# Two fp32r activation halves in one 512-column matmul

## The chip, the cores and the metric

The kernel runs on one core of one Trainium2 chip. The metric is the time of one execution on the device in microseconds; the median of three runs of the kernel before is 2723.91 us (2716.98 to 2725.1).

## The reference

Two transformer blocks of depth 2 follow each other on 256 tokens of width 1024, in fp32. The first has a pooling and gating mixer in its layer 0 and sparse attention with retention in layer 1. The second has adaptive normalisation (nine rows of shifts, scales and gates for each layer, from a vector `c` times `ada_w`), differential attention in layer 0 and grouped attention in layer 1, and carries a second stream, the context, beside x. Every mixer stands between linear layers, and FFNs do most of the work:

```python
def swiglu_2(h, w_in, w_out):
    gate, up = jnp.split(h @ w_in, 2, axis=-1)
    return (jax.nn.silu(gate) * up) @ w_out

def half_ffn(h, m, k, g_pre, g_post, w_in, w_out):
    y = swiglu_2(modulated_norm(h, g_pre, m, k), w_in, w_out)
    return gated_residual(h, y, g_post, m, k, 0.5)
```

The hidden width is 2816. x goes through six FFNs (called gu0 to gu5 below), the context through three (gu2, gu3, gu4).

## The kernel before

**The split product.** Features lie on the 128 partitions and the 256 tokens (`T`) along the free axis. TensorE multiplies in fp32r, which keeps fewer bits than fp32, so each fp32 operand is split in a high part (rounded to fp32r) and a low part (the rest), and a product is the sum of three: high by high, high by low, low by high. `product` (L264) issues one matmul: `w` picks high or low weights (`WHI`, `WLO`), `xp` the high or low activations (`S.HN` or `S.G`, two tensors each). `three` issues the three for each of the k tiles of 128 features, one after the other into the same 256 columns of a PSUM bank. Three such matmuls are called a triple here.

**Weights.** A block is 128 x 2048: eight k tiles of two output tiles of 128 features. SyncE loads blocks into four raw slots in the order of `plan`; a load waits until the block four places ahead is done. `splits` (L223, L230, L243) lets ScalarE copy a raw block to `WHI` (three buffers) and VectorE subtract it in two halves to give `WLO`. The split of block n+2 or n+3 is issued in the middle of block n, between its two output tiles.

**Lanes.** x and the context are two lanes (`X`, `C`), generators whose steps a hand-written scheduler puts in one order: each engine runs its instructions in that order. Beside them a third generator, `modulation`, makes the shifts and gains from 72 blocks of `ada_w` (L1115, L1129). In gu5 x is alone; in the other FFNs context or modulation blocks stand between x's blocks.

**An FFN of x.** For each of 11 pairs (256 hidden features) a gate block goes to bank 0 (both output tiles side by side) and an up block to bank 1. ScalarE takes tanh of the gate bank to `TMP` (L446), VectorE forms the gate (L448), which frees the bank, then multiplies by the up bank (L461), which frees that; ScalarE writes the high part of the result to `GX_hi` (L465), VectorE the low part (L467). The first pair is made by `first_blocks`, which starts while the norm is still making the high and low parts, tile by tile: for each k the two products on the high activations, one tile later that on the low ones, and from k = 5 on the second block as well. The down projection takes, for each pair of output tiles, 22 k tiles in three blocks of 6, 8 and 8, into the first halves of two banks.

**Outputs.** `put_out` takes each of the eight output tiles of a down or output projection (`ev_out`, `od_out`, `da_out`, `ga_out`): ScalarE squares it twice and copies it to `Y`, each with the PSUM bank as its input (L352, L355, L356), and VectorE adds up the sums for the norm (L366 to L372). Then `norm` makes the inverse root with small matmuls (L538, L553) and writes `HN` (L686 to L700). Its banks are 2 and 3.

**Counts.** Input projections have 6 (ev), 14 (od, one of them with a single output tile), 12 (da) and 6 (ga) blocks for x; output projections four each; each FFN 22 gate and up blocks and 12 down blocks.

Of the kernel before, what the change touches and what calls it, by code (L numbers as in the profile page):

```python
# [9 lines left out]
P = 128  # L10
D = 1024
KD = D // P
T = 256
# [28 lines left out]
Mark = namedtuple("Mark", "sem n")  # L42

# [40 lines left out]
def build(nc, A, out):  # L84
# [4 lines left out]
    with ExitStack() as ctx:  # L89
        def sb(name, shape, dt=fp32):  # L90
            return ctx.enter_context(nc.sbuf_tensor(name, shape, dt))

        HX, HC = sb("HX", [P, KD, T]), sb("HC", [P, KD, T])
# [6 lines left out]
        with ExitStack() as g:  # L100
            HNX = [g.enter_context(nc.sbuf_tensor(f"HNX_{n}", [P, KD, T], f32r)) for n in ("hi", "lo")]
            GX = [g.enter_context(nc.sbuf_tensor(f"GX_{n}", [P, KF, T], f32r)) for n in ("hi", "lo")]
# [4 lines left out]
        HNC = [sb(f"HNC_{n}", [P, KD, T], f32r) for n in ("hi", "lo")]  # L107
        with ExitStack() as g:
            GC = [g.enter_context(nc.sbuf_tensor(f"GC_{n}", [P, 8, T], f32r)) for n in ("hi", "lo")]
# [16 lines left out]
        BANK = [ctx.enter_context(nc.psum_tensor(f"bank{n}", [P, 512], fp32)) for n in range(8)]  # L126
# [5 lines left out]
            "total", "root", "rstd", "scaled", "resid", "normed", "hn_hi", "hn_lo")]  # L132
        for n in names:
            sems[n] = ctx.enter_context(nc.semaphore(n))
# [8 lines left out]
        def carve(arena, at, end):  # L143

            def piece(n, *dims, dt=None):
# [11 lines left out]
                if len(dims) == 2:  # L157
# [5 lines left out]
                 (BANK[2], BANK[3], BANK[0], BANK[1]), (BANK[0], BANK[1]), (BANK[3], BANK[4]), BANK[2], BANK[3], False, False)  # L163
# [11 lines left out]
        def program(pe=None, act=None, dve=None, pool=None, sp=None):  # L175
# [90 lines left out]

            def three(dst, n, col, x, ks, start, stop, waits=None):
# [48 lines left out]
            def first_blocks(S, n, dst, hi, lo):  # L316


                LAG = 5
                landed(n)  # L320
                for j in range(KD + LAG):
                    for m in range(2):
                        if j < KD and on(pe, None if m else hi[j]):
                            for w in range(2):
                                product(dst[0][:, m * T:(m + 1) * T], n, m * P, j, S.HN, 0, j, w, j == 0 and m == 0 and w == 0, False, True)
                    for m in range(2):
                        if 1 <= j <= KD and on(pe, None if m else lo[j - 1]):
                            mm = product(dst[0][:, m * T:(m + 1) * T], n, m * P, j - 1, S.HN, 1, j - 1, 0, False, j == KD, True)
                            if j == KD and m == 1:
                                mm.then_inc(sems["block_done"], 1)  # L330
                    if j == LAG:
                        splits(n)
                        landed(n + 1)
                    for m in range(2):
                        for w, xp in ((0, 0), (1, 0), (0, 1)) if j >= LAG and pe else ():
                            k = j - LAG
                            mm = product(dst[1][:, m * T:(m + 1) * T], n + 1, m * P, k, S.HN, xp, k, w, k == 0 and m == 0 and (w, xp) == (0, 0),
                                         k == KD - 1 and xp == 1, True)
# [6 lines left out]
            def put_out(S, src, k, gain, *ready):  # L345

                t, first = S.tag, k == 0
                sq, gg, ev = up(f"{t}_sq"), up(f"{t}_gg"), up(f"{t}_evac")
                if on(act, *ready, *((*free.get((t, "sums"), ()), *free.get((t, "gain"), ())) if first else ())):
# [12 lines left out]
                else:  # L362
# [6 lines left out]
                    if on(dve, ev, hs0):  # L369
                        NV.tensor_tensor(part, S.H[:, k, :], S.Y[:, k, :], MUL).then_inc(hg.sem, 1)  # L370
                        dve.wait_ge(*hg)
                        NV.tensor_tensor(S.HG, S.HG, part, ADD).then_inc(hs.sem, 1)  # L372
                return ev

            def linear(S, name, blocks, dst, ready=(), first=None, gain=None):
# [3 lines left out]
                if first is not None:  # L379
# [5 lines left out]
                    first_blocks(S, n, S.pair, *first)  # L385
                for j, (b, at, *alone) in enumerate(blocks):
                    tiles = 1 if alone else 2
                    if first is None or j >= 2:
# [4 lines left out]
                        if gain is not None and not S.lag:  # L393
                            banks = S.tiles[2 * (j % 2)], S.tiles[2 * (j % 2) + 1]
                            dsts = banks[0][:, 0:T], banks[1][:, 0:T]
# [7 lines left out]
                    def job(banks=banks, at_n=at_n, at=at, tile=tile, tiles=tiles):  # L403
                        if gain is not None:
                            for m in range(2):
                                src = banks[m][:, 0:T] if not S.lag else halves(banks[m])[m]
                                free[banks[m].name] = put_out(S, src, at + m, gain, done(at_n) if m or S.lag else tile)
                            marks.append(free[banks[1].name])
# [8 lines left out]
                return marks  # L417

            def ffn(S, which, gain, first):
# [6 lines left out]
                for c, pairs in enumerate(chunks):  # L426
                    for p in pairs:
                        gate, up_ = S.pair
                        if p == 0 and not S.chunked:
                            yield ("F",)  # L430
                            n = take(t, "w_main", base)
                            take(t, "w_main", base + 1)
                            on(pe, free.get(gate.name), free.get(up_.name))
                            first_blocks(S, n, S.pair, *first)
                            ng, nu = n, n + 1
                        else:
                            yield ("D",)
                            ng = take(t, "w_main", base + 2 * p)
                            on(pe, *(first[1] if p == 0 else ()), free.get(gate.name))
                            yield from two_tiles(S, ng, halves(gate), S.HN, ALL, True, True)  # L440
                            nu = None
# [9 lines left out]
                        if nu is None:  # L451
                            yield ("D",)
                            nu = take(t, "w_main", base + 2 * p + 1)
                            on(pe, free.get(up_.name))
                            yield from two_tiles(S, nu, halves(up_), S.HN, ALL, True, True)
                        kt = 2 * p - 8 * c if S.chunked else 2 * p

                        def keep(p=p, nu=nu, kt=kt, down_done=down_done):
# [4 lines left out]
                            g = [x[:, kt:kt + 2, :].rearrange("p a b -> p (a b)") for x in S.G]  # L463
                            if on(act, ud, down_done):
                                NS.activation(g[0], S.TMP[p % 2][:, :], ACT.Copy).then_inc(hi.sem, 1)  # L465
                            if on(dve, hi):
                                NV.tensor_tensor(g[1], S.TMP[p % 2][:, :], g[0].bitcast(fp32), SUB).then_inc(lo.sem, 1)  # L467
# [7 lines left out]
                    if not S.chunked:  # L475
                        for mp in range(4):
                            banks = S.tiles[2 * (mp % 2)], S.tiles[2 * (mp % 2) + 1]
                            for cc, (k0, k1) in enumerate(SHORT_FIRST):
# [7 lines left out]
                                yield from two_tiles(S, n, [b[:, 0:T] for b in banks], S.G, ks, cc == 0, cc == 2, waits, tile, 2, mp == 3 and cc == 2)  # L486
                            for m in range(2):
                                free[banks[m].name] = put_out(S, banks[m][:, 0:T], 2 * mp + m, gain, done(n) if m else tile)
# [1597 lines left out]
```

## Time and profile before

| | |
|---|---|
| median of three runs | 2723.91 us (2716.98 to 2725.1) |
| span of the profiled execution | 2725.8 us |
| time of the profiled execution beside its span | none is given; the three runs are those above |
| instructions in it | 48854 |
| TensorE, weight loads | 93%, 88% of the span |
| VectorE, ScalarE | 63%, 46% |
| mean granted TensorE clock | 0.966 |
| read from HBM | 471.48 MB, 173 GB/s |

The span runs from the first to the last instruction. A matmul's recorded duration is longer than the distance to the next one, since matmuls are pipelined; the distance between starts is what a stream of them costs.

### The profile page before, as it was taken

The page shows a single profiled execution, that of the slowest core. Times are in us where ns is not written, and L with a number is a line of the kernel's source. Part 1 is how long each engine was busy: PE and PEld are TensorE (multiplying, and loading weights), DVE is VectorE, ACT ScalarE, POOL GpSimd, SP SyncE. Part 2 cuts the span into 40 slices and gives each one's busy share as a digit, 9 for nine tenths or more (in the row PEclk, how much of TensorE's full clock was granted, in tenths as well). Part 3 has the DMA queues.
Part 4 walks back from the last instruction along what each step waited for, and adds up shares of the span by engine and source line. Part 5 has one row for each costly group of instructions (what it writes and reads, how often), then busy time and mean ns, then how long its engine had stood idle before and what let it go on. Part 6 is the DMA issues. An engine that isn't in the chain of part 4 may idle for free.

```text
span 2725.8 us, 48854 instructions
## 1 busy us (share of the span) xinstructions
PE 2528.6 (93%) x20780; PEld 2395.9 (88%) x20780; DVE 1707.1 (63%) x2804; ACT 1248.6 (46%) x1697; POOL 1.2 (0%) x6
## 2 busy tenths in 40 slices
PE   6799997999999999999888998999999999887998
PEld 5689996888998999999887898999999999756997
DVE  6565574656766565566767576577655557646655
ACT  4443453444544444445445554455444345435443
POOL 0000000000000000000000000000000000000000
PEclk9899999999999999999898999999999999888999
DMA  6456656533555665544351344555545555363453
GB/s 218 181 200 242 241 203 229 189 109 124 186 202 216 236 226 196 211 147 154 132 174 52 120 171 154 185 175 173 179 170 179 180 177 183 114 215 137 170 178 116
DMA packets 71591, 480.14 MB, mean 176 GB/s; under 512 B 8784, under 2 KB 9296, under 8 KB 17744
## 3 DMA queue, kind: packets, MB, share of 16 engines
q1 hardware_dynamic: 66240, 468.74, 48.8%
q10 hardware_dynamic: 5136, 8.28, 1.0%
q8 instruction: 166, 2.72, 0.4%
q14 instruction: 49, 0.40, 0.0%
HBM read 471.48 MB, written 1.05 MB: 173 GB/s over the span
## 4 chain that ended last, share of the span: by engine, by line
PE 73%; DVE 13%; ACT 7%; DMA 4%; issue 3%; ACTq 0%; DVEq 0%
PE bank L264 64%; ACT whi L223 4%; DVE wlo L243 2%; DMA raw<-w_main 2%; DVE wlo L230 2%; PE bank L1115 2%; DMA raw<-w_down 1%; PE bank L997 1%; PE bank L935 1%; DVE ARX L686 1%; DVE HX L637 1%; DVE tmpx L631 1%; PE bank L985 1%; PE bank L553 0%; PE bank L1639 0%
## 5 line engine op out<-in xcount | busy, mean ns | idle before, releaser
L264 PE MATMUL bank<-HNX_hi,whi 128*128 128x256 f32 x2968 | 866.2, 293 | 64.3 <-DVE wlo L243 24.4
L223 ACT ACTIVATE whi<-raw 128x2048 fp32r<-128x2048 f32 (+1 forms) x378 | 705.5, 1868 | 334.6 <-PE bank L264 149.4
L264 PE MATMUL bank<-HNX_hi,wlo 128*128 128x256 f32 x2968 | 849.8, 287 | 0.0
L264 PE MATMUL bank<-HNX_lo,whi 128*128 128x256 f32 x2968 | 834.6, 286 | 0.0
L230 DVE TENSOR_TENSOR wlo<-raw,whi 128x1024 fp32r<-128x1024 f32 (+1 forms) x378 | 453.4, 1199 | 570.1 <-ACT whi L223 569.5
L264 PEld LDWEIGHTS bank<-HNX_hi,whi 128*128 128x128 f32 x2968 | 582.4, 196 | 91.7 <-issue 50.7
L264 PEld LDWEIGHTS bank<-HNX_hi,wlo 128*128 128x128 f32 x2968 | 583.1, 196 | 0.0
L264 PEld LDWEIGHTS bank<-HNX_lo,whi 128*128 128x128 f32 x2968 | 573.2, 196 | 1.1 <-issue 0.9
L243 DVE TENSOR_TENSOR wlo<-raw,whi 128x1024 fp32r<-128x1024 f32 (+1 forms) x378 | 450.8, 1193 | 0.0
L264 PE MATMUL bank<-HNC_hi,whi 128*128 128x256 f32 x1344 | 390.2, 290 | 11.6 <-DVE tmpc L448 4.5
L264 PE MATMUL bank<-HNC_lo,whi 128*128 128x256 f32 x1344 | 381.7, 284 | 0.0
L264 PE MATMUL bank<-HNC_hi,wlo 128*128 128x256 f32 x1344 | 381.6, 284 | 0.0
L264 PE MATMUL bank<-GX_hi,whi 128*128 128x256 f32 x1056 | 302.6, 287 | 4.0 <-DVE wlo L243 3.9
L264 PE MATMUL bank<-GX_lo,whi 128*128 128x256 f32 x1056 | 298.7, 283 | 0.0
L264 PE MATMUL bank<-GX_hi,wlo 128*128 128x256 f32 x1056 | 298.6, 283 | 0.0
L264 PEld LDWEIGHTS bank<-HNC_hi,whi 128*128 128x128 f32 x1344 | 259.2, 193 | 22.5 <-issue 7.9
L264 PEld LDWEIGHTS bank<-HNC_lo,whi 128*128 128x128 f32 x1344 | 259.4, 193 | 0.6 <-issue 0.2
L264 PEld LDWEIGHTS bank<-HNC_hi,wlo 128*128 128x128 f32 x1344 | 259.2, 193 | 0.0
L264 PEld LDWEIGHTS bank<-GX_hi,whi 128*128 128x128 f32 x1056 | 202.4, 192 | 10.4 <-DVE wlo L243 7.8
L264 PEld LDWEIGHTS bank<-GX_lo,whi 128*128 128x128 f32 x1056 | 202.5, 192 | 0.1
L264 PEld LDWEIGHTS bank<-GX_hi,wlo 128*128 128x128 f32 x1056 | 202.4, 192 | 0.0
L465 ACT ACTIVATE GX_hi<-tmpx 128x512 fp32r<-128x512 f32 x66 | 41.7, 632 | 250.0 <-DVE tmpx L461 250.0
(349 smaller groups left out, 2923.7 us busy)
## 6 DMA issues: line engine op xcount, KB each, us to landing
raw<-w_main SPq DMA_DIRECT2D x270, 1024.0 KB, 4.8
raw<-w_ada SPq DMA_DIRECT2D x72, 1024.0 KB, 4.8
raw<-w_down SPq DMA_DIRECT2D x72, 1024.0 KB, 4.9
raw<-w_down SPq DMA_DIRECT2D x36, 768.0 KB, 4.2
raw<-w_cmp SPq DMA_DIRECT2D x4, 1024.0 KB, 4.8
tmpx<-ARX ACTq DMA_DIRECT2D x18, 128.0 KB, 4.8
tmpx<-ARX ACTq DMA_DIRECT2D x32, 64.0 KB, 4.7
HX<-x_in SPq DMA_DIRECT2D x2, 512.0 KB, 6.0
```

Source lines behind the costliest of these rows:

```text
L223: NS.activation(WHI[q % HIS][:, 0:size], RAW[m % SLOTS][:, 0:size], ACT.Copy).then_inc(sems["w_hi"], 1)
L230: NV.tensor_tensor(WLO[m % SLOTS][:, 0:half], RAW[m % SLOTS][:, 0:half], WHI[q % HIS][:, 0:half].bitcast(fp32), SUB)
L243: NV.tensor_tensor(WLO[m % SLOTS][:, half:size], RAW[m % SLOTS][:, half:size], WHI[q % HIS][:, half:size].bitcast(fp32), SUB).then_inc(sem ...
L264: return NT.matmul(dst, (WHI[ordinal[n] % HIS], WLO[n % SLOTS])[w][:, k * 2 * P + col:k * 2 * P + col + P], x[xp][:, kx, :], start=start, ...
L465: NS.activation(g[0], S.TMP[p % 2][:, :], ACT.Copy).then_inc(hi.sem, 1)
L631: NV.tensor_tensor(S.TMP[k % 2][:, 0:T], S.Y[:, k, :], S.wide_y[:, 0:T], MUL).then_inc(sc.sem, 1)
L637: NV.tensor_tensor(S.H[:, k, :], S.H[:, k, :], S.TMP[k % 2][:, 0:T], ADD).then_inc(re.sem, 1)
L686: NV.scalar_tensor_tensor(S.Y[:, k, :], S.H[:, k, :], gain(k), S.wide_h[:, 0:T], MUL, MUL).then_inc(no.sem, 1)
L935: mm = NT.matmul(bank[:, c0 + c * T:c0 + (c + 1) * T], q[pr, :], k[pr, :], start=True, stop=True)
L985: mm = NT.transpose(turn_bank[:, c * P:(c + 1) * P], PB[w % 3][:, 0, c * P:(c + 1) * P], ident)
L997: mm = NT.matmul(out_bank[:, 0:P], v, PT[b][:, c * P:(c + 1) * P], start=c == 0, stop=c == len(vs) - 1)
L1115: mm = NT.matmul(bank[32 * g:32 * g + 32, 0:T], CCOL[:, k, 6 - 2 * r:38 - 2 * r], RAW[n % SLOTS][:, k * T:(k + 1) * T], start=r == 0 and k ...
```

## The change

The high and low activations become one tensor `[P, k, 2, T]`, so that for each k the two halves lie next to each other, 512 columns. For x's gate, up, down and output projections the three matmuls become two: low weights by high activations (256 columns, into a bank's first half, "main"), and high weights by both halves at once (512 columns: high by high adds to main, high by low goes to the second half, "cross"). Each output tile now has a bank of its own: gate in banks 0 and 1, up in banks 2 and 3. The norm's banks of x move to 3 and 4. Before anything else reads an output, ScalarE copies cross to SBUF and VectorE adds main to it; the instructions of old then read that sum in SBUF, and the banks are free after the add. x's input projections and everything of the context keep three matmuls. In `first_blocks` the wide matmul waits for the low half, and ahead of the second block there is a new wait, for bank 3.

```diff
+            def high_by_both(dst, n, col, k, x, kx, stop, loose=False):
+                return NT.matmul(dst, WHI[ordinal[n] % HIS][:, k * 2 * P + col:k * 2 * P + col + P], x.both[:, kx, :, :].rearrange("p a b -> p (a b)"),
+                                 start=False, stop=stop, skip_group_check=loose)
...
-                    if on(pe, *(waits or {}).get(kx, ())):
+                    if on(pe, *(waits or {}).get(kx, ())) and is_wide(dst):
+                        product(dst[:, 0:T], n, col, k, x, 0, kx, 1, start and j == 0, False, True)
+                        mm = high_by_both(dst, n, col, k, x, kx, stop and j == len(ks) - 1, True)
+                    elif pe:
                         for w, xp in ((0, 0), (0, 1), (1, 0)):
...
                     for m in range(2):
                         if j < KD and on(pe, None if m else hi[j]):
+                            if wide:
+                                product(dst[0][m][:, 0:T], n, m * P, j, S.HN, 0, j, 1, j == 0, False, True)
...
                         if 1 <= j <= KD and on(pe, None if m else lo[j - 1]):
+                            if wide:
+                                mm = high_by_both(dst[0][m], n, m * P, j - 1, S.HN, j - 1, j == KD, True)
...
                     if j == LAG:
                         splits(n)
                         landed(n + 1)
+                        on(pe, free.get(S.wide_y.name))
...
+                if not S.lag:
+                    bank, src, summed = src, S.Y[:, k, :], up("x_tile_sum")
+                    apart = up("x_cross")
+                    if on(act, *ready):
+                        NS.activation(src, bank.cross(), ACT.Copy).then_inc(apart.sem, 1)
+                    if on(dve, apart):
+                        NV.tensor_tensor(src, bank.main(), src, ADD).then_inc(summed.sem, 1)
+                    ready = (summed,)
...
+                if on(act, done(ng), held.get(p % 2)):
+                    NS.activation(made, PS[:, 0:2, T:2 * T], ACT.Copy).then_inc(gc.sem, 1)
+                if on(dve, gc):
+                    NV.tensor_tensor(gate, PS[:, 0:2, 0:T], made, ADD).then_inc(gs.sem, 1)
+                if on(act, gs):
+                    NS.activation(made, gate, ACT.Tanh, scale=0.5).then_inc(th.sem, 1)
+                if on(dve, th):
+                    NV.scalar_tensor_tensor(made, made, 1.0, gate, ADD, MUL).then_inc(act_.sem, 1)
+                free[gates[0].name] = free[gates[1].name] = gs
...
+                if on(act, done(nu)):
+                    NS.activation(up_, PS[:, 2:4, T:2 * T], ACT.Copy).then_inc(uc.sem, 1)
+                if on(dve, uc, act_):
+                    NV.tensor_tensor(up_, PS[:, 2:4, 0:T], up_, ADD).then_inc(us.sem, 1)
+                    dve.wait_ge(*us)
+                    NV.scalar_tensor_tensor(made, made, 0.5, up_, MUL, MUL).then_inc(ud.sem, 1)
+                free[ups[0].name] = free[ups[1].name] = us
```

## Rows read from the trace of the kernel before

**Rows 1.** The page: busy time by engine; the granted clock in 40 slices.

```profile
PE 2528.6 (93%) x20780; PEld 2395.9 (88%) x20780; DVE 1707.1 (63%) x2804; ACT 1248.6 (46%) x1697; POOL 1.2 (0%) x6
...
PEclk9899999999999999999898999999999999888999
```

**Rows 2.** The page's groups: count, busy us, mean ns, idle us before.

```profile
L264 PE MATMUL bank<-HNX_hi,whi 128*128 128x256 f32 x2968 | 866.2, 293 | 64.3 <-DVE wlo L243 24.4 <-ACT HNX_hi L691 16.5 <-ACT HNX_hi L689 12.8
...
L264 PE MATMUL bank<-HNC_hi,whi 128*128 128x256 f32 x1344 | 390.2, 290 | 11.6 <-DVE tmpc L448 4.5 <-DVE HNC_lo L700 4.2 <-DVE HNC_lo L842 1.4
...
L264 PE MATMUL bank<-GX_hi,whi 128*128 128x256 f32 x1056 | 302.6, 287 | 4.0 <-DVE wlo L243 3.9
```

**Rows 3.** Timeline in gu5, full clock: start us, duration us, instruction.

```profile
2590.00 0.28 PE L264 MATMUL bank<-HNX_hi,whi 128*128 128x256 f32 x1
2590.12 0.28 PE L264 MATMUL bank<-HNX_lo,whi 128*128 128x256 f32 x1
...
2590.12 0.19 PEld L264 LDWEIGHTS bank<-HNX_hi,wlo 128*128 128x128 f32 x1
```

**Rows 4.** Windows (PEclk after the engines) and timeline at the lower clock.

```profile
142.00:144.00 2.00, 2.00 (x10) 1.93 (x10) 2.00 (x7) 0.66 (x2) 0.00 (x0) 0.50 0.00 0
...
142.90 0.41 PE L264 MATMUL bank<-HNX_hi,whi 128*128 128x256 f32 x1
143.11 0.41 PE L264 MATMUL bank<-HNX_hi,wlo 128*128 128x256 f32 x1
```

**Rows 5.** Timelines of one-column matmuls and of plain fp32 matmuls, merged.

```profile
665.63 1.05 PE L793 MATMUL bank<-VEC,tmpx 128*128 128x1 f32 x8 [0.82 <-ACT tmpx L786]
666.54 0.36 PE L264 MATMUL bank<-GC_hi,whi 128*128 128x256 f32 x1
...
2412.00 0.59 PE L935 MATMUL bank<-KC,ARX 128*128 128x256 f32 x2
2412.43 0.59 PE L935 MATMUL bank<-ARX 128*128 128x256 f32 x2
```

**Rows 6.** Timeline of ScalarE and of VectorE over one pair of gu5.

```profile
2584.80 0.60 ACT L446 ACTIVATE tmpx<-bank 128x512 f32<-128x512 f32 x1 [2.60 <-PE bank L264]
2585.29 1.91 ACT L223 ACTIVATE whi<-raw 128x2048 fp32r<-128x2048 f32 x1
2591.28 0.63 ACT L465 ACTIVATE GX_hi<-tmpx 128x512 fp32r<-128x512 f32 x1 [4.08 <-DVE tmpx L461]
...
2596.32 0.60 ACT L446 ACTIVATE tmpx<-bank 128x512 f32<-128x512 f32 x1 [2.60 <-PE bank L264]
...
2585.43 0.69 DVE L448 SCALAR_TENSOR_TENSOR tmpx<-tmpx,bank 128x512 f32<-128x512 f32 x1 [0.84 <-ACT tmpx L446]
2587.23 1.23 DVE L230 TENSOR_TENSOR wlo<-raw,whi 128x1024 fp32r<-128x1024 f32 x1 [1.12 <-ACT whi L223]
2588.37 1.22 DVE L243 TENSOR_TENSOR wlo<-raw,whi 128x1024 fp32r<-128x1024 f32 x1
```

**Rows 7.** Timeline of ScalarE in gu0, with modulation blocks between.

```profile
263.48 0.60 ACT L446 ACTIVATE tmpx<-bank 128x512 f32<-128x512 f32 x1 [2.60 <-PE bank L264]
...
276.18 0.60 ACT L446 ACTIVATE tmpx<-bank 128x512 f32<-128x512 f32 x1 [2.60 <-PE bank L264]
```

**Rows 8.** Groups of 128x256 that read a bank.

```profile
L352 ACT ACTIVATE sqx<-bank 128x256 f32<-128x256 f32 x70 | 26.9, 384 | 79.1 <-PE bank L264 79.1
...
L631 DVE TENSOR_TENSOR tmpx<-ARX,bank 128x256 f32<-128x256 f32 x80 | 32.2, 413 | 2.5 <-PE bank L553 2.3
```

**Rows 9.** Timeline of TensorE after ga_out: the norm's sums.

```profile
2508.43 0.44 PE L538 MATMUL bank<-sumxy,VEC 128*32 128x64 f32 x8 [3.63 <-DVE sumxy L366]
```

**Rows 10.** Windows of gu5 and gu0 (last: DMA share, GB/s); loads, us to landing.

```profile
2520.00:2640.00 120.00, 117.98 (x975) 117.37 (x975) 73.40 (x85) 51.75 (x45) 0.00 (x0) 1.00 0.50 171
240.00:290.00 50.00, 49.68 (x440) 46.75 (x440) 26.10 (x29) 18.95 (x18) 0.00 (x0) 1.00 0.69 249
...
raw<-w_main SPq DMA_DIRECT2D x270, 1024.0 KB, 4.8
```

More of the change, by code:

```diff
@@ L42, with __getitem__, main, cross @@
 Mark = namedtuple("Mark", "sem n")
+Split = namedtuple("Split", "hi lo both")
+@dataclass
+class Bank:
+    name: str
+    ap: Any
+    def __getitem__(self, key):
+        return self.ap[key]
+    def main(self):
+        return self.ap[:, 0:T]
+    def cross(self):
+        return self.ap[:, T:2 * T]
 class Between:
@@ L125, in build @@
         ROWS = sb("rows", [P, T])
-        BANK = [ctx.enter_context(nc.psum_tensor(f"bank{n}", [P, 512], fp32)) for n in range(8)]
+        PS = ctx.enter_context(nc.psum_tensor("bank", [P, 8, 512], fp32))
+        BANK = [Bank(f"bank{n}", PS[:, n, :]) for n in range(8)]
         sems = {}
@@ L319, in first_blocks @@
                 LAG = 5
+                wide = is_wide(dst[0][0])
                 landed(n)
@@ L372, in put_out @@
                         NV.tensor_tensor(S.HG, S.HG, part, ADD).then_inc(hs.sem, 1)
+                if not S.lag:
+                    free[bank.name] = summed
                 return ev
@@ L384, in linear @@
                         on(pe, free.get(b.name))
-                    first_blocks(S, n, S.pair, *first)
+                    first_blocks(S, n, [halves(b) for b in S.pair], *first)
                 for j, (b, at, *alone) in enumerate(blocks):
@@ L428, in ffn @@
                         gate, up_ = S.pair
[L429 to L441, printed above, removed]
+                        if not S.chunked:
+                            yield from wide_pair(S, p, base, first, gain, held, lo_marks)
+                            continue
+                        yield ("D",)
+                        ng = take(t, "w_main", base + 2 * p)
+                        on(pe, *(first[1] if p == 0 else ()), free.get(gate.name))
+                        yield from two_tiles(S, ng, halves(gate), S.HN, ALL, True, True)
                         def silu(p=p, ng=ng):
@@ L450, in ffn @@
                         after(S, silu)
[L451 to L456, printed above, removed]
+                        yield ("D",)
+                        nu = take(t, "w_main", base + 2 * p + 1)
+                        on(pe, free.get(up_.name))
+                        yield from two_tiles(S, nu, halves(up_), S.HN, ALL, True, True)
+                        kt = 2 * p - 8 * c
                         def keep(p=p, nu=nu, kt=kt, down_done=down_done):
@@ L476, in ffn @@
                         for mp in range(4):
[L477 removed]
+                            banks = S.tiles[mp % 2]
                             for cc, (k0, k1) in enumerate(SHORT_FIRST):
@@ L485, in ffn @@
                                 tile = up(f"{t}_tile") if cc == 2 else None
-                                yield from two_tiles(S, n, [b[:, 0:T] for b in banks], S.G, ks, cc == 0, cc == 2, waits, tile, 2, mp == 3 and cc == 2)
+                                yield from two_tiles(S, n, [b[:, :] for b in banks], S.G, ks, cc == 0, cc == 2, waits, tile, 2, mp == 3 and cc == 2)
                             for m in range(2):
-                                free[banks[m].name] = put_out(S, banks[m][:, 0:T], 2 * mp + m, gain, done(n) if m else tile)
+                                put_out(S, banks[m], 2 * mp + m, gain, done(n) if m else tile)
                         continue
```

81 lines of the change are left out of this document (62 added, 19 removed).

## Prediction

> **What bounds the kernel now.** I read the page first: TensorE is busy 93% of the span, VectorE 63%, ScalarE 46%, and the granted clock is nine tenths or more in all but six of its 40 slices [rows 1]. The groups by line then show that one line, the split product, holds nearly all matmuls, that they come in equal thirds, and that the idle time ahead of them is small: 64.3 us ahead of the largest group, 11.6 and 4.0 ahead of two others [rows 2]. So in most stretches TensorE's own pace sets the time. What is that pace? The timeline inside a dense stretch shows a new 256-column matmul every 0.12 us, each with a weight load of its own [rows 3]. The stretch has the full clock, 2.4 GHz; 256 columns at one column per cycle are 106.7 ns, so each matmul costs 13.3 ns over its columns. What these 13.3 ns hang on decides this change.
>
> **What is removed, and what one triple gains.** A triple (three loads, three 256-column matmuls, 768 columns) becomes a pair (two loads, 256 + 512 columns, again 768 columns). No column is saved: only a load and what is paid per matmul. Triples that change: the x down projections, 1056, and of the 2968 over HNX all but those of the input projections, which keep the old form: 6+14+12+6 blocks of 16, less 8 of a half block, 600. That leaves 2368 + 1056 = 3424. At the lower clock level the pitch is 0.21 us, which is just 256 columns at 1.2 GHz, so nothing is saved there [rows 4]; I take 5% off for it, an estimate from the clock's slices [rows 1], and work with 3250.
>
> The trace has no split product of 512 columns, so the price is bounded. Above: a one-column matmul with its load takes 0.91/8 = 0.114 us, so loading alone fills nearly the whole pitch of 0.12 [rows 5]. If the load sets the pitch, it hides wholly under 512 columns; two 256-column matmuls of plain fp32 follow each other at 0.43/2 = 0.215 us [rows 5], about 512 columns' time at 2.4 GHz, and I take that for the wide one. The pair is 0.120 + 0.216 = 0.336, the gain 24 ns, 78 us in all. Below: if the 13.3 ns belong to the columns (operands that arrive at 0.469 ns a column whatever the load does), the pair is 0.360 and the gain nothing. Between: 13.3 ns are paid once per matmul, 0.120 + 0.227 = 0.347, the gain 13.3 ns, 43 us. I take the middle: the plain fp32 row shows that a long stream under one load pays almost nothing extra, and no row shows wide operands streaming at full rate.
>
> Here the Trainium skill ("TensorE: Matmul & The Clock Gate", section "Back-to-back issue gap") has a rule that speaks against the change: a warm matmul follows the last after columns/2.4 plus about 2.5 ns. For 256 columns that is 109 ns, and [rows 3] show 120, so the trace does not agree. By that rule alone a triple would go from 327 to 325 ns and the change would give 8 us at most. The same page's section on LDWEIGHTS gives columns/1.2, 107 ns for 128 columns; [rows 5] show 114 for a matmul that is little else, close to it.
>
> **What is added.** Each x tile now goes ScalarE copy, VectorE add, and then the old chain.
>
> FFN pairs (66): two ScalarE copies of 128x512 at about 0.60 and two VectorE adds at 0.69, as tanh and the product cost [rows 6]: 79 and 91 us. Most lies under matmuls, since both engines have room [rows 1]. But the chain is longer and both queues are in order. Follow one pair in the stretch where x runs alone (gu5). Before, ScalarE's tanh starts at 2584.80, the whi copy follows at 2585.29, wlo is split at 2587.23, and VectorE waits only for those [rows 6]. After, the loop on the two queues is: add 0.72, tanh 0.49 (0.60 less what the next instruction overlaps), whi 1.94, two wlo halves 2 x 1.14, then for the up half add 0.64, product 0.72, high part 0.54, whi 1.94 and wlo 2.28 again: 11.5 us a pair (handoffs of 0.03 are in). TensorE's pair is 11.52 before (2584.80 to 2596.32) and 32 x 0.347 = 11.1 after. So in gu5 the loop is slower than the new TensorE. Weights are split ahead of use, with 3 to 4 us in hand, so of ten pairs' 0.45 us each about 1 us comes through; at 0.336 it is 10 x 0.8 less the same, 4 to 5. Elsewhere a modulation block stretches the pair to 12.7 us (263.48 to 276.18) [rows 7], a context block by more, and the loop is hidden.
>
> Tails: after the last matmul of an x down or output projection, the norm waits for one more copy (0.38), add (0.42) and two handoffs: 0.8 us [rows 8]. There are ten such places, and nothing covers them in full: TensorE waits 3.63 us ahead of one norm's sums [rows 9], and 16.5 and 12.8 us in all for the high parts that the norms make [rows 2]. 8 us. In the output projections each block of 5.5 us now asks of the two queues two tiles of about 1.8 us, whi 1.9 and, ahead of the next tile's add, wlo 2.3: 7.6 in place of under 6. Queues fall behind; in ga_out, which runs almost alone and already ends with VectorE late [rows 9], I count 4 us, in the other three, with context or modulation work between, 1.3 each: 8. In the down projections a block pair lasts 15.8 us, so only 0.5 at the end: 3. The opening product of each FFN now keeps its high weights for the low half, and waits in its middle for bank 3, which the norm frees with its last residual: 0.3 a time, 2.
>
> Weights: with modulation blocks between, the loads run at 249 GB/s against 171 in gu5 [rows 10]. A raw slot is freed four blocks ahead, and one of the three blocks between is a modulation block of about 1 us, so load and split stand against some 12.5 us of TensorE work. A load lands 4.8 us after its issue at the median [rows 10]; two issued together I estimate at up to 9, plus 1.9 and 2.3 for the split, 13. A faster TensorE runs into that. About a third of the changed triples lie in such stretches, and I take a third of their gain away: 5 us. Context attention chains that share the two busier queues: 2.
>
> **The sum.** 43 - 8 (tails) - 8 (output projections) - 3 - 2 - 1 - 5 - 2 = +14 us. The profiled span is 2725.8; no time of that execution is given beside it, and it is 1.9 above the median of 2723.9. The sum goes on the median: 2710.
>
> **Rivals.**
> (a) The load sets the pitch. For it: the one-column matmul at 0.114, and that loads and matmuls start together [rows 3, 5]. Against: 0.114 is not 0.120. Gain 78; losses grow to about 38, since gu5 loses 5 and the fed stretches 9: net +40, 2684.
> (b) Slower: the extra time belongs to the columns. For it: the plain fp32 matmul, whose 256 columns take twice as long, shows no such extra, and at the lower clock the extra is gone [rows 4, 5], as if operands came at a fixed speed that only the full clock outruns. Against: nothing shows it at 512 columns. Gain nothing; the losses that stay are the tails, the projections and the contention, 20 to 23: net -20, 2744. It decides once a triple gains less than about 7 ns (23 us over 3250). The gap rule of the Trainium skill named above would end here too.
> (c) Slower: the loop of ScalarE and VectorE becomes the bound in all FFN stages and not in gu5 alone. For it: 11.5 against 11.1. Against: VectorE is 63% busy, and the pairs elsewhere are longer [rows 1]. 66 x 0.45 = 30 us lost from +14: 2740.
>
> **Chances.** Forecast 0.38 (its own range 2697 to 2722), (a) 0.27, (b) 0.30, (c) 0.05. The range reaches from (a) to (b): 2677 to 2746. About 0.3%, 8 us, is what a measurement of this kernel can tell from no change. Faster: all of (a) and seven tenths of the forecast's spread, 0.53. Same: 0.16, from the forecast's weak end and (b)'s good end. Slower: 0.31.
>
> **What would show it.** The timeline of a dense x stretch: the wide matmul's distance to the next start, 0.227 (forecast), 0.216 (a), 0.240 (b), with 0.120 for the narrow one. The copy and add groups should read 132 ScalarE and 132 VectorE instructions of 128x512 near 0.60 and 0.69, and 80 each of 128x256 near 0.4. In gu5, TensorE should start to wait for wlo late in the stage, and the chain of waits should hold more VectorE. TensorE's idle ahead of the norm's sums should grow by about 1 us each, by more in ga_out. I am wrong if the wide pitch is near 0.24, if TensorE waits for wlo in every FFN, or if the pitch of the unchanged context triples moves.

## The result, and the profile after

The changed kernel takes 2805.6 us (2804.09 to 2816.4), the kernel before beside it on the same chip 2720.44: a ratio of 1.0325, 95% interval 1.0301 to 1.0349. It is 85 us slower. 2710 was forecast, in a range of 2677 to 2746. I was wrong by 96 us, and on the side to which I had given 0.31.

The page of the changed kernel: busy time by engine, the granted clock in 40 slices, the chain that ended last, and groups as in [rows 2]. The split product has two lines now, `product` (L287) and `high_by_both` (L293).

```profile
PE 2519.5 (90%) x17356; PEld 2214.0 (79%) x17356; DVE 1834.2 (65%) x3016; ACT 1356.8 (48%) x1909; POOL 1.2 (0%) x6
...
PEclk9899999999999999999898999999999999888999
...
PE 53%; DVE 23%; ACT 14%; issue 6%; DMA 3%; ACTq 1%; DVEq 0%
...
L287 PE MATMUL bank<-HNX,wlo 128*128 128x256 f32 x2968 | 849.6, 290 | 58.4 <-DVE wlo L266 28.7
L293 PE MATMUL bank<-HNX,whi 128*128 128x512 f32 x2368 | 844.8, 401 | 0.0
...
L287 PE MATMUL bank<-GX,wlo 128*128 128x256 f32 x1056 | 305.5, 289 | 19.0 <-DVE wlo L266 19.0
L287 PE MATMUL bank<-HNX,whi 128*128 128x256 f32 x1200 | 235.2, 296 | 29.6 <-DVE wlo L266 15.8
```

Against [rows 1]: 3424 matmuls are gone, VectorE has 127 us more work and ScalarE 108. Neither is near full. TensorE's busy time says little between kernels with different matmuls (recorded durations overlap). What moved is the waiting: ahead of the matmuls over `HNX` 64.3 us of idle time stood before [rows 2], now 58.4 + 29.6; ahead of those over `GX` 4.0 before and 19.0 now, all of it for `wlo`, VectorE's low weights.

Did the wide matmul do what it should? The timeline of a stretch without waits, in the run e2 (below), which has the same matmuls: start us, duration us.

```profile
2599.80 0.39 PE L293 MATMUL bank<-HNX,whi 128*128 128x512 f32 x1
2600.03 0.28 PE L287 MATMUL bank<-HNX,wlo 128*128 128x256 f32 x1
2600.15 0.39 PE L293 MATMUL bank<-HNX,whi 128*128 128x512 f32 x1
...
2601.88 0.39 PE L293 MATMUL bank<-HNX,whi 128*128 128x512 f32 x1
```

A wide matmul is followed after 0.23 us and a narrow one after 0.12. These starts are rounded to 10 ns, so the pair is better read over several: six pairs lie between 2599.80 and 2601.88, 0.347 us each, and 437 pairs between 2520 and 2670 us have the same mean. With 0.120 for the narrow matmul, 0.227 is left for the wide one. The triple takes 0.360 (466 of them in the trace of before, 2535 to 2700 us). That is a gain of 13.3 ns a triple, just what was forecast. Over all of e2's some 3000 pairs at the full clock the mean is 0.349, a gain of 11 ns.

The copies and adds, grouped by shape:

```profile
L515 DVE TENSOR_TENSOR ARX<-bank,ARX 128x512 f32<-128x512 f32 x66 | 45.5, 689 | 47.6 <-ACT ARX L513 47.0
L500 DVE TENSOR_TENSOR ARX<-bank,tmpx 128x512 f32<-128x512 f32 x66 | 45.3, 687 | 21.3 <-ACT tmpx L498 21.3
L502 ACT ACTIVATE tmpx<-ARX 128x512 f32<-128x512 f32 x66 | 41.7, 632 | 97.0 <-DVE ARX L500 97.0
...
L401 DVE TENSOR_TENSOR ARX<-bank,ARX 128x256 f32<-128x256 f32 x80 | 33.6, 420 | 25.4 <-ACT ARX L399 25.4
L399 ACT ACTIVATE ARX<-bank 128x256 f32<-128x256 f32 x80 | 29.8, 373 | 52.7 <-PE bank L293 52.3
L406 ACT ACTIVATE sqx<-ARX 128x256 f32<-128x256 f32 x70 | 29.2, 417 | 89.5 <-DVE ARX L401 89.5
```

Counts and durations are those forecast. New are the last columns of the tanh (L502) and the square (L406): ScalarE stands still for 97.0 and 89.5 us because VectorE has not added yet. Before, the same square waited 79.1 us, and for TensorE [rows 8]. Such idle time is no loss by itself: in the kernel before, ScalarE also stood 250.0 us ahead of `GX_hi` (L465) for VectorE's product. It costs something where TensorE waits in the end. Three of TensorE's waits grow most. They are shown in the changed kernel and then in e2, which has the same matmuls without copies and adds (total us, number of waits, longest):

```profile
PE bank L287 <- DVE wlo L266: 69.6, 49, 4.8
PE bank L1120 <- ACT ARC L1159: 21.2, 8, 3.8
PE bank L639 <- ACT ARX L410: 20.7, 5, 7.9
```

```profile
PE bank L287 <- DVE wlo L266: 31.0, 23, 3.5
PE bank L1108 <- ACT ARC L1147: 5.0, 4, 1.6
PE bank L627 <- DVE sumxy L414: 7.5, 2, 4.0
PE bank L627 <- ACT ARX L404: 2.9, 3, 1.3
```

The low weights hold TensorE up for 39 us more, context attention's copy for 16, the norm's sums for 10: 65 of the 79 us by which TensorE's idle time grows (span less busy time, 285.2 against 206.2). The other 32 us of the 110.6 between the two spans are busy time, 2519.5 against 2487.9 for the same matmuls. Most of that can be the clock: its mean is 0.957 here and 0.966 in e2, which makes at most 0.043 x 2804.7 - 0.034 x 2694.1 = 29 us (an estimate; part of the lower clock falls in waits).

One place for each kind of wait shows how it comes about.

**The end of ga_out.** ScalarE, then VectorE, in the changed kernel; in brackets the idle time and what ended it.

```profile
2579.91 1.90 ACT L246 ACTIVATE whi<-raw 128x2048 fp32r<-128x2048 f32 x1
2581.71 0.37 ACT L399 ACTIVATE ARX<-bank 128x256 f32<-128x256 f32 x1
2584.78 0.42 ACT L406 ACTIVATE sqx<-ARX 128x256 f32<-128x256 f32 x1 [2.70 <-DVE ARX L401]
...
2587.28 0.42 ACT L406 ACTIVATE sqx<-ARX 128x256 f32<-128x256 f32 x1 [1.02 <-DVE ARX L401]
```

```profile
2582.06 1.22 DVE L253 TENSOR_TENSOR wlo<-raw,whi 128x1024 fp32r<-128x1024 f32 x1
2583.19 1.22 DVE L266 TENSOR_TENSOR wlo<-raw,whi 128x1024 fp32r<-128x1024 f32 x1
2584.33 0.42 DVE L401 TENSOR_TENSOR ARX<-bank,ARX 128x256 f32<-128x256 f32 x1
...
2586.49 0.42 DVE L426 TENSOR_TENSOR sumxg<-sumxg,tmpx 128x256 f32<-128x256 f32 x1
2586.83 0.42 DVE L401 TENSOR_TENSOR ARX<-bank,ARX 128x256 f32<-128x256 f32 x1
```

The copy of the first tile is ready at 2582.08, but its add stands behind the two halves of a split until 2584.33. The second tile's add stands behind the four sums of the first. TensorE then waits for the norm's sums:

```profile
2588.59 0.44 PE L639 MATMUL bank<-sumxy,VEC 128*32 128x64 f32 x8 [7.92 <-ACT ARX L410]
```

It was 3.63 before [rows 9]: 4.3 us more. For this place the prediction had 0.8 (tail) and 4 (ga_out), 4.8 in all, so its size was right here.

**Context attention in gu2.** A context block's score matmuls wait for a ScalarE copy. After, 21.2 us in all (above); the group before, and then one of these places after:

```profile
L1019 PE MATMUL bank<-KC,ARC 64*128 64x256 f32 x64 | 11.2, 426 | 4.3 <-ACT ARC L1058 4.3
```

```profile
1312.12 0.42 ACT L406 ACTIVATE sqx<-ARX 128x256 f32<-128x256 f32 x1 [1.02 <-DVE ARX L401]
...
1313.24 1.89 ACT L246 ACTIVATE whi<-raw 128x2048 fp32r<-128x2048 f32 x1
1315.05 0.36 ACT L1159 ACTIVATE ARC<-bank 128x256 f32<-128x256 f32 x1
...
1315.77 1.23 PE L1120 MATMUL bank<-KC,ARC 64*128 64x256 f32 x4 [3.78 <-ACT ARC L1159]
```

The copy that attention needs (L1159) comes after the whole chain of an output tile and after the weight split behind it.

**gu1, with modulation and the context's norm between.** ScalarE, VectorE and TensorE merged, in the changed kernel:

```profile
923.15 0.69 DVE L515 TENSOR_TENSOR ARX<-bank,ARX 128x512 f32<-128x512 f32 x1 [0.66 <-ACT ARX L513]
923.88 0.69 DVE L517 SCALAR_TENSOR_TENSOR tmpx<-tmpx,ARX 128x512 f32<-128x512 f32 x1
924.61 0.63 ACT L521 ACTIVATE GX<-tmpx 128x512 fp32r<-128x512 f32 x1 [1.48 <-DVE tmpx L517]
925.14 1.89 ACT L246 ACTIVATE whi<-raw 128x2048 fp32r<-128x2048 f32 x1
...
925.63 1.07 PE L1216 MATMUL bank<-raw,CCOL 128*32 128x256 f32 x16
...
927.07 1.23 DVE L253 TENSOR_TENSOR wlo<-raw,whi 128x1024 fp32r<-128x1024 f32 x1 [1.11 <-ACT whi L246]
...
930.12 1.22 DVE L266 TENSOR_TENSOR wlo<-raw,whi 128x1024 fp32r<-128x1024 f32 x1
931.49 0.55 PE L287 MATMUL bank<-HNX,wlo 128*128 128x256 f32 x1 [4.79 <-DVE wlo L266]
931.84 0.63 PE L293 MATMUL bank<-HNX,whi 128*128 128x512 f32 x1
...
932.48 0.63 PE L293 MATMUL bank<-HNX,whi 128*128 128x512 f32 x1
```

The high weights (925.14) start when the up half's chain is through, so the low ones are late and TensorE waits 4.79 us. The same place before:

```profile
901.35 1.90 ACT L223 ACTIVATE whi<-raw 128x2048 fp32r<-128x2048 f32 x1
...
905.08 1.07 PE L1115 MATMUL bank<-raw,CCOL 128*32 128x256 f32 x16
907.70 0.36 PE L264 MATMUL bank<-HNX_hi,whi 128*128 128x256 f32 x1 [1.55 <-DVE wlo L243]
```

Five instructions of the context's norm stand between the halves of the low weights in both kernels (after: from 928.21 to 930.12). What differs is the start of the high weights: 3.73 us ahead of the modulation block's matmuls before, 0.49 now. The 3.24 us between are the 3.24 by which the wait grew.

Behind the longer wait the clock is at its lower level, 1.2 GHz (0.50 granted from 931 to 934): the pair takes 0.64 us (931.84 to 932.48), as a triple does there [rows 4], and the change gains nothing. Behind the wait of 1.55 us before, it stayed at the full level (1.00 from 907 to 910).

### The profile page after: what moved, and what is told of

It is laid out like the page before. It is cut to its first block, busy times and chain, and to the rows that moved or that the text cites. A ratio compares the mean times of both kernels' runs of the same rounds, so it can differ in the third digit from the quotient of the medians.

```text
span 2804.7 us, 42440 instructions
## 1 busy us (share of the span) xinstructions
PE 2519.5 (90%) x17356; PEld 2214.0 (79%) x17356; DVE 1834.2 (65%) x3016; ACT 1356.8 (48%) x1909; POOL 1.2 (0%) x6
## 4 chain that ended last, share of the span: by engine, by line
PE 53%; DVE 23%; ACT 14%; issue 6%; DMA 3%; ACTq 1%; DVEq 0%
PE bank L287 31%; PE bank L293 15%; ACT whi L246 8%; DVE wlo L266 6%; DVE wlo L253 4%; DMA raw<-w_main 2%; PE bank L1216 1%; DVE tmpx L517 1%; PE bank L1098 1%; DVE ARX L515 1%; ACT ARX L410 1%; ACT diagx L409 1%; PE bank L1036 1%; DVE ARX L787 1%; DMA tmpx<-ARX 1%
## 5 line engine op out<-in xcount | busy, mean ns | idle before, releaser
L287 PE MATMUL bank<-HNX,wlo 128*128 128x256 f32 x2968 | 849.6, 290 | 58.4 <-DVE wlo L266 28.7
L293 PE MATMUL bank<-HNX,whi 128*128 128x512 f32 x2368 | 844.8, 401 | 0.0
L287 PEld LDWEIGHTS bank<-HNX,wlo 128*128 128x128 f32 x2968 | 575.0, 195 | 88.1 <-issue 49.8
L293 PEld LDWEIGHTS bank<-HNX,whi 128*128 128x128 f32 x2368 | 450.2, 192 | 96.9
L287 PE MATMUL bank<-HNC,whi 128*128 128x256 f32 x2688 | 500.4, 288 | 17.8 <-DVE tmpc L549 8.0
L287 PEld LDWEIGHTS bank<-HNC,whi 128*128 128x128 f32 x2688 | 424.2, 193 | 30.7 <-issue 9.9
L287 PE MATMUL bank<-HNC,wlo 128*128 128x256 f32 x1344 | 382.1, 284 | 0.0
L293 PE MATMUL bank<-GX,whi 128*128 128x512 f32 x1056 | 380.3, 401 | 0.0
L287 PE MATMUL bank<-GX,wlo 128*128 128x256 f32 x1056 | 305.5, 289 | 19.0 <-DVE wlo L266 19.0
L287 PE MATMUL bank<-HNX,whi 128*128 128x256 f32 x1200 | 235.2, 296 | 29.6 <-DVE wlo L266 15.8
L287 PEld LDWEIGHTS bank<-HNC,wlo 128*128 128x128 f32 x1344 | 258.9, 193 | 0.0
L293 PEld LDWEIGHTS bank<-GX,whi 128*128 128x128 f32 x1056 | 203.0, 192 | 45.6
L287 PEld LDWEIGHTS bank<-HNX,whi 128*128 128x128 f32 x1200 | 197.1, 200 | 40.7 <-issue 22.8
L287 PEld LDWEIGHTS bank<-GX,wlo 128*128 128x128 f32 x1056 | 204.7, 194 | 27.0 <-DVE wlo L266 24.3
L287 PE MATMUL bank<-GC,whi 128*128 128x256 f32 x1056 | 197.2, 288 | 5.7 <-DVE wlo L266 5.7
L287 PEld LDWEIGHTS bank<-GC,whi 128*128 128x128 f32 x1056 | 167.0, 192 | 11.7 <-issue 10.5
L287 PE MATMUL bank<-GC,wlo 128*128 128x256 f32 x528 | 150.2, 284 | 0.0
L287 PEld LDWEIGHTS bank<-GC,wlo 128*128 128x128 f32 x528 | 101.4, 192 | 0.0
```

Source lines behind the costliest of these rows:

```text
L287: return NT.matmul(dst, (WHI[ordinal[n] % HIS], WLO[n % SLOTS])[w][:, k * 2 * P + col:k * 2 * P + col + P], x[xp][:, kx, :], start=start, ...
L293: return NT.matmul(dst, WHI[ordinal[n] % HIS][:, k * 2 * P + col:k * 2 * P + col + P], x.both[:, kx, :, :].rearrange("p a b -> p (a b)"), ...
```

## The experiments

Each kernel is compared with the kernel before on the same chip; differences are against that, unless another is named. Two theories stood at the start: the wide matmul costs the time, or the chain behind it does.

**e1: the chain without the wide matmul.**

```diff
-                return NT.matmul(dst, WHI[...][...], x.both[:, kx, :, :]..., start=False, stop=stop, ...)
+                product(dst[:, 0:T], n, col, k, x, 0, kx, 0, False, stop, True)
+                return product(dst[:, T:2 * T], n, col, k, x, 1, kx, 0, False, stop, True)
```

> Every wide matmul is two of 256 columns again (high by high into main, high by low into cross); banks, copies, adds and waits stay as in the changed kernel. Chain theory (the copy and the add make ScalarE and VectorE late, and the wide matmul is a gain of about 34 us, since the traces show pairs of 0.350 us in place of triples of 0.360): 2810 to 2840, no faster than the changed kernel's 2806. Matmul theory (the wide matmul or its two halves of a bank cost the time): 2720 to 2740.

2822.7 us, ratio 1.0373 [1.0356, 1.039]: +102. The matmul theory falls. Even beside the late chain the wide matmul saves 17 us (102 less 85).

**e2: the wide matmul without the chain.**

```diff
-                        NS.activation(src, bank.cross(), ACT.Copy).then_inc(apart.sem, 1)
-                        NV.tensor_tensor(src, bank.main(), src, ADD).then_inc(summed.sem, 1)
+                    bank, src, summed = src, src.main(), ev
```

(and so for the gate and the up half)

> Wide matmuls and the new banks stay, but nobody reads cross: the copies and adds are left out, and tanh, product and squares read main in the bank as before, so the output lacks the cross sums. Chain theory: the gain of the matmuls alone, 2720 - 34 = 2686, at most 2700. Matmul theory: 2790 to 2806.

2696.5, ratio 0.9903 [0.9886, 0.9921]: -24. So the chain costs 85 + 24 = 109 us. e2 is the base for e6, e7, e9, e10 and e13.

**e3 and e4: gate and up alone, down and output projections alone.**

> Only the gate and up projections are wide (with their copies and adds); down and output projections have their three matmuls and old chain. By the points where the delay grows in the changed kernel (gu0, gu1, gu2 with attention beside it), the gate and up part holds some 55 of the 79 us: 2765 to 2780. If the outputs' chain (five instructions on each tile) is the main cause: 2720 to 2735.

> The other half: only down and output projections are wide, with the copy and add of each output tile; gate and up are as before. If the parts add up: 2805 - (e3 - 2720), about 2745. If the outputs' chain is the main cause: 2780 to 2790.

e3: 2758.9, ratio 1.0137 [1.0122, 1.0152], +38. e4: 2775.1, ratio 1.0198 [1.0183, 1.0213], +54.5. Both lie outside their ranges. Both halves lose, and I had the larger one wrong: with 80 tiles of 256 columns against 132 instruction pairs of 512, and less than half of the triples, the outputs lose more. The sum is 92.8, not 85; the new layout (e17) is in both.

**e5: the same instructions in another order.** After the copy and the add, the rest of a chain goes behind the next split of weights.

```diff
+                def rest():
+                    if on(act, gs):
+                        NS.activation(made, gate, ACT.Tanh, scale=0.5).then_inc(th.sem, 1)
...
+                late.append(rest)
```

> The same instructions as the changed kernel in another order in ScalarE's and VectorE's queues: after the copy and the add, the rest of each chain (tanh and product of the gate; product, high and low part of the up half; squares, gained copy and sums of an output tile) is put behind the next split of weights. Queue theory (the loss is the weight split and attention's copies standing behind a chain that hops between the two engines): 2750 to 2780. Work theory (each added instruction costs its own time wherever it stands): within 10 us of the changed kernel's 2806.

2768.8, ratio 1.0172 [1.0155, 1.0189], +48: 37 of the 85 us were a matter of order. (The up half's add also drops its wait for the gate's product, which stands ahead of it in VectorE's queue anyway.) In the trace the tanh's 97.0 us of idle time are down to 16.8, the square's 89.5 only to 76.3.

```profile
L517 ACT ACTIVATE tmpx<-ARX 128x512 f32<-128x512 f32 x66 | 41.2, 624 | 16.8 <-DVE ARX L514 16.8
...
L416 ACT ACTIVATE sqx<-ARX 128x256 f32<-128x256 f32 x70 | 28.9, 413 | 76.3 <-DVE ARX L410 76.3
```

**e6 and e7: copies alone, adds alone.**

```diff
+                    if on(dve, *ready):
+                        NV.tensor_tensor(src, bank.main(), S.H[:, k, :], ADD).then_inc(summed.sem, 1)
```

(e7's; e6 keeps the copy and reads main in the bank)

> As the kernel without copies and adds (2696), but ScalarE's 212 copies are back, into places that nobody reads; no adds, cross sums left out. Work theory: copies and adds share the 109 us that the chain costs about as their busy times do, so 2696 + 45 to 55 = 2745. Queue theory: the copy without a hop to VectorE costs far less than half, 2705 to 2725.

> As the changed kernel, but no copies: VectorE's add takes main and the residual stream from SBUF in place of cross, so the cross sums are left out. Work theory: 2696 + 55 to 65 = 2755. Queue theory: the hop to VectorE and back is there but one step shorter than in the changed kernel: 2735 to 2755, and copy alone and add alone together stay 30 us or more below the 109 of both.

e6: 2712.1, ratio 0.9958 [0.9946, 0.997], 15 us over e2. e7: 2793.8, ratio 1.0264 [1.0247, 1.0281], 97 over e2; I had expected 2755 at most. The copies, which raise ScalarE's busy time from 1248.9 us (e2) to 1339.5, cost 15. At the gate and the output tiles nothing waits for them; at the up half VectorE's product does. The adds cost nearly everything. But work or detour? And that copy alone and add alone together reach the 109 of both was not in the queue theory as I had put it.

**e8: gu2 and its down projection as before**, the rest changed.

> The changed kernel with one of the six FFNs of x as before: gu2 and its down projection, which run beside context attention. By the points of the trace where the delay grows (29 us at the 216th load, 58 at the 240th): 30 us less, 2775. If the loss follows the number of added instructions, a sixth of the FFNs' share: 2790 to 2795.

2784.9, ratio 1.0234 [1.0219, 1.025], +64: 21 us of the 85 come back, net of the gain that gu2's own wide matmuls lose: more than a sixth (14), less than the 30 that I read from how the issue of the same weight load shifts between the two traces (the 240th: 1323.14 us before, 1381.53 after).

**e9 and e10: the detour without the work, the work without the detour.**

```diff
+                    if on(dve, *ready):
+                        NV.tensor_tensor(S.Y[:, k, 0:1], src[:, 0:1], S.H[:, k, 0:1], ADD).then_inc(small.sem, 1)
+                    ready = (small,)
```

(e9's, at the output tiles; the gate has the same)

> As the kernel without copies and adds (2696), but tanh of a gate and the squares of an output tile wait for a one-column instruction of VectorE on the same bank: the detour over VectorE's queue without its work. Detour theory (what costs 97 us in e7 is that ScalarE waits for VectorE's queue, where weight splits stand): 2740 to 2780. Work theory (VectorE's 117 us of adds stand ahead of its weight splits): 2700 to 2715.

> As the kernel without copies and adds (2696), but VectorE makes all 212 adds at full size, after ScalarE has read the bank, and nobody reads or waits for their results: the work without the detour. Work theory: 2760 to 2790. Detour theory: 2705 to 2730.

e9: 2742.7, ratio 1.0089 [1.0075, 1.0103], 47 us over e2. e10: 2723.4, ratio 1.0008 [0.9999, 1.0018], 28 over e2. In e10 ScalarE's square waits 76.2 us, and for TensorE. In e9, the groups of the square and of VectorE's one-column instruction at the output tiles:

```profile
L404 ACT ACTIVATE sqx<-bank 128x256 f32<-128x256 f32 x70 | 26.9, 385 | 124.8 <-DVE ARX L399 124.8
L399 DVE TENSOR_TENSOR ARX<-bank,HX 128x1 f32<-128x1 f32 x80 | 12.2, 153 | 18.1 <-PE bank L293 18.0
```

146 instructions of 0.15 us, 22 us of work, cost more than the adds whose results nobody reads, by which VectorE's busy time grows from e2's 1707.0 us to 1810.2. (In e10 an output tile's bank is still released only behind its add, so its 28 us are not the work alone.) What e9 adds is the wait for a place in VectorE's queue. The two together make 75 of e7's 97; the other 22 come only when both are there.

The Trainium skill says it in "PSUM — Partial Sum Buffer", section "Engine vs sequencer instructions": the queues of ScalarE and VectorE are strictly first in, first out. The rows agree: the add of 2584.33 above had its input at 2582.08 and waited for the halves of `wlo` that were issued before it.

**e11: VectorE relieved by GpSimd**, which makes the FFN's low parts and most of the norm sums.

> The changed kernel with VectorE relieved of other work: GpSimd, idle before, makes the low part of the FFN's result and the norm sums of the first six output tiles. Work theory: VectorE loses about as much work as the adds brought, so 2730 to 2770, unless GpSimd is so slow that the down projection waits for its low parts. Detour theory: 2790 to 2810, since tanh and the squares still wait for VectorE's splits.

2801.3, ratio 1.0303 [1.0287, 1.0319]: +82, 3 us better, with intervals that overlap. The page shows that VectorE is down to 1722.5 us of work, near its 1707.1 in [rows 1]. Fewer busy microseconds did not help. GpSimd takes 1298 ns for a low part that VectorE makes in 693, so a part of the relief may be lost in its chains; the run does not separate that. VectorE's halves of the weight split also take a little longer beside it, 1250 and 1238 ns in place of 1225 and 1219.

**e12: only what paid.** Gate and up wide in gu3, gu4 and gu5, in e5's order; all else as before.

> A version that keeps only what paid: gate and up wide in gu3, gu4 and gu5 alone, with the order of e5; down and output projections and gu0 to gu2 as before. e3's trace loses nothing there and gains 1 to 3 us in each: 2712 to 2717, a ratio of 0.997 to 0.999.

2714.4 (11 runs; 21 of before), ratio 0.9981 [0.9972, 0.999]: 5 us faster than the kernel before, inside the 0.3% that I called no change, but with an interval that leaves out 1.

**e13: the detour at the output tiles alone**, as in e9 without the gates.

> e9 with the one-column detour only at the 80 output tiles of down and output projections; the gates' tanh waits for the matmuls alone. If the detour costs at the output tiles: 2730 to 2743, nearly all of e9's 46 us over 2696. If it costs in the FFN pairs: 2697 to 2712.

2727.2, ratio 1.0025 [1.001, 1.0041], 32 us over e2 and between the two ranges: two thirds of e9's 47 are the output tiles'.

**e14: both adds first.**

```diff
+                ev = next(a)
...
+                ev = next(b)
+                late.append(lambda: (next(a), next(a), next(b), next(b)))
```

(`a` and `b` are `put_out` of the two tiles; the first step issues the copy and the add)

> e5 with one more change of order: for the two output tiles of a block pair both copies and both adds stand ahead of the squares and the four sums of the first. If the second tile's add behind the first tile's sums matters (ScalarE waits 1.02 us for it at each pair in the changed kernel's timeline, 40 pairs): 2735 to 2760. If not: within 6 us of e5's 2769.

2755.2, ratio 1.0131 [1.0111, 1.015], +36: 12 us more come back. The square's idle time falls from e5's 76.3 us to 27.8. TensorE's wait for attention's copy was 21.2 us in the changed kernel, 11.2 in e5, and is 5.6 here.

```profile
L416 ACT ACTIVATE sqx<-ARX 128x256 f32<-128x256 f32 x70 | 28.7, 410 | 27.8 <-DVE ARX L408 27.8
```

**e15: down projections alone, in that order.**

> The order of e14 with the down projections alone wide; gate, up and output projections as before. If order was the trouble: 1056 triples gain 8 us and the six tails lose 5 to 8, 2715 to 2730. If the add costs wherever it stands: 2740 to 2755 (e4, down and output projections in the first order, is 2775).

2743.1, ratio 1.0088 [1.0071, 1.0104], +24. My expectation fell: with the best order that I found, the 1056 triples with most matmuls to an add still lose. Order was about half of the trouble (49 of 85 us), not all. What the rest hangs on is open.

**e16: e12 with the down projections of gu4 and gu5.**

> e12 (2714) with the down projections of gu4 and gu5 wide as well, in the order of e14. 352 more triples gain 3 us, two tails lose 2: 2711 to 2717. If the add at output tiles costs in gu4 and gu5 too: 2718 to 2726.

2714.6, ratio 0.9989 [0.9977, 1.0001]: no better than e12. e12 stays the only version with all its sums whose interval lies under 1.

**e17: the rest of the change.** All products narrow and all chains old.

> The changed kernel with all its projections back to three narrow matmuls and the old chains; what stays is the merged tensor of the two halves, the norm's banks 3 and 4, and the wait for bank 3. If these are free: 2718 to 2722. By the prediction's term: 2 us, 2722. If the chips' gain of 24 us in e2 hides a cost of the layout: 2726 or more.

2725.8 (12 runs; 17 of before), ratio 1.0027 [1.0015, 1.0039]: +4.7 by the medians, 7 by the ratio. The layout is not free. Which of its three parts costs this stays open: the profiled span is 2719.8, below that of before, so the traces do not show it.

## Why the prediction was wrong, point by point

**The matmuls.** The mechanism was right, and so was the price in a dense stretch: 0.227 for the wide matmul and 13.3 ns a triple. Only the sum was a little large: 43 us booked, less the 5 for loads that a faster TensorE runs into; e2 against e17 gives 24.1 + 4.7 = 29 us by the medians (8.9 ns over 3250 triples) and 34 by the ratios; the whole run's mean of 11 ns would make 36. Rivals (a), 0.216 for the wide matmul, and (b), 0.240, both fall. The Trainium skill's rule ("TensorE: Matmul & The Clock Gate", section "Back-to-back issue gap"), which that section gives for a matmul by itself and by which a wide one takes 216 ns and the change gives 8 us, does not fit: 227 was measured, and 120 where it has 109.

**The step that failed** is the cost of what is added: "Most lies under matmuls, since both engines have room", with "handoffs of 0.03". I summed durations along a loop and let a handoff cost what it costs between idle engines. But an instruction that waits for the other engine waits for that engine's queue, 1.02 to 2.70 us in the rows above, and the weight split and attention's copy behind it wait too. All terms of the chain together (tails 8, output projections 8, gu5 1, down 3, attention 2) were 22 us; measured, 109 (the 5 for loads belong to the gain, and are in e2). Against e2 the copies alone cost 15, the adds' work alone 28 and the detour alone 47; the rest comes only when they meet.

**Term by term.** Tails: the idle time ahead of the norm's sums in x's ten norms is 20.7 us after (the line of L639 above), 9.9 before. That is 10.8 more where the tails' 8 and the 4 of ga_out were booked: about right.

```profile
L538 PE MATMUL bank<-sumxy,VEC 128*32 128x64 f32 x80 | 3.4, 247 | 9.9 <-DVE sumxy L366 9.6 <-issue 0.3
```

gu5, which I worked out with most care, came out close: in 200 us that hold gu5's gate, up and down blocks, TensorE waits 2.4 us ahead of its largest narrow group, where 1 was booked, though the tanh waits 26.7 us for VectorE.

```profile
L287 PE MATMUL bank<-HNX,wlo 128*128 128x256 f32 x346 | 97.4, 284 | 2.4 <-DVE ARX L500 2.2
...
L502 ACT ACTIVATE tmpx<-ARX 128x512 f32<-128x512 f32 x11 | 7.0, 632 | 26.7 <-DVE ARX L500 26.7
```

How the delay grows shows the same. Of the 378 copies of high weights, in order, those after start 5 us late at 186 us (of the kernel before), 31 at 1139, 58 at 1328, 69 at 1897, 83 at 2551, and 81 at 2653. In gu5 the changed kernel catches up a little; 28 us arise in the 190 in which gu2 and context attention share the queues.

What failed was the sentence "Elsewhere a modulation block stretches the pair to 12.7 us (...), a context block by more, and the loop is hidden". A longer pair holds other work for the same two queues. With 8.9 ns a triple as the gain (an estimate from e2 and e17), e3's gate and up blocks cost 38 + 19 = 57 us, where 1 was booked for the pairs; e4's outputs cost 54.5 + 12 = 66, where the tails, the output projections and the down projections had 19. Attention was booked at 2: TensorE's waits for its copy alone grew by 16.9 us, and e8 got 21 back. Down projections were booked at 3, and their six tails at 5; e15, in a better order and with their gain counted, is still 24 slower, at most 4.7 of it the layout's. The opening product's 2 us for bank 3 are within e17's 4.7, not separated.

One slip in the working changes no term: the queues' work for a block of an output projection, two tiles of 1.8 with 1.9 and 2.3, is 7.8 us and not 7.6.

**Rival (c)**, ScalarE and VectorE as the bound in all FFNs, was nearest in kind and had 0.05. It had the wrong reason: neither engine is the bound by its work (65% and 48% busy; e11 takes 112 us of work away and gains 3), but their queues are by their order (e5 and e14 give 49 us back). Of my signs of being wrong, "if TensorE waits for wlo in every FFN" came closest to what happened: 49 waits after, 23 in e2.

## What to carry to other kernels

When a change puts an instruction of one engine between two of another, price it by what stands in that engine's queue at that moment, not by its duration: here a one-column detour cost more (47 us) than 103 us of adds whose results nobody read (28). Count then what stands behind the waiting instruction, and look in the stretches where other lanes use the same queues; the stretch that is easiest to work out, where one lane runs alone, is the one where it costs least. A busy share of 65% says that the work fits, and nothing of when it is done.

## What the runs showed of the hardware that I had not expected

A 512-column fp32r matmul behind a 128-column load of its own is followed after 0.227 us; its two halves as two matmuls take 0.240. At one column a cycle of 2.4 GHz, 256 columns are 106.7 ns and 512 are 213.3, so both lengths pay the same 13.3 ns once per matmul, and twice the columns do not pay twice. What it is spent on no run shows.

At the lower clock level a pair takes 0.64 us, a triple's time, so a wait behind which the clock is lower, as that of 4.79 us in gu1, also takes the change's gain away for the stretch behind it. The mean granted clock is 0.957 after and 0.966 before.
